# Recurrence of a hybrid decoder step: two squares written with their heads exchanged, summed on the other two 64x64 tiles

## What is computed

```python
kk = k * k_k.astype(f32).reshape(H, N)
kk = kk / jnp.maximum(jnp.sqrt(jnp.sum(kk * kk, axis=-1, keepdims=True)), 1e-12)
...
o, S = _wkv7_scan(S0.astype(f32), r, decay, k, v, kk, a)
mean = jnp.mean(o, axis=-1, keepdims=True)
var = jnp.mean(jnp.square(o - mean), axis=-1, keepdims=True)
o = ((o - mean) * lax.rsqrt(var + LNX_EPS) * lnx_g + lnx_b)
o = o + jnp.sum(r * k * r_k.astype(f32), axis=-1, keepdims=True) * v
```

## Time and profile before

| | us |
|---|---|
| median of 3 runs | 1933.91 |
| lowest and highest of the 3 | 1926.66 and 1935.87 |
| the profiled execution, its own time | 1932.09 |
| its span from the first to the last instruction | 1930.1 |
| busy: PE, PEld, DVE, ACT, POOL | 1802.9, 1538.8, 1049.6, 798.0, 249.6 |
| mean granted clock of TensorE, share of full speed | 0.985 |
| first and last sum over `sq` | 498.9 and 758.9 |
| start of the first `csq`, and of the last | 555.4 and 814.7 |
| `sq`: 16 instructions of ACT, median each | 0.552 |
| `csq`: 16 instructions of ACT, median each | 0.462 |
| one 64x64 weight load, median | 0.135 |
| from one `ss` to the next: a steady slot (643.53 to 659.88) | 16.35 |
| the same for the one long slot among them (607.63 to 627.19) | 19.56 |

### The profile page before, as it was taken

How to read it: one execution, slowest core, us unless ns; L and a number is a source line. 1 busy time by engine, 2 the same in 40 slices (tenths; PEclk the granted TensorE clock), 3 DMA queues, 4 the chain that set the end, 5 groups by cost and what they waited for, 6 DMA issues and landing times.

```text
span 1930.1 us, 43901 instructions
## 1 busy us (share of the span) xinstructions
PE 1802.9 (93%) x18432; PEld 1538.8 (80%) x18432; DVE 1049.6 (54%) x1718; ACT 798.0 (41%) x1459; POOL 249.6 (13%) x315
## 2 busy tenths in 40 slices
PE   7999999999999999999998998999999998778797
PEld 6988999999888888799986776777776776334697
DVE  6744464453588999444445533443463445676334
ACT  4234233233466767333333323233343444555233
POOL 0300000000245555232000000000000001010032
PEclk9999999999999999999999999999999999998899
DMA  8534554555355553243889999999999999999541
GB/s 295 185 142 156 179 180 155 170 179 165 92 137 139 142 137 97 92 141 143 340 292 417 420 419 409 414 426 425 426 426 417 414 425 380 418 393 364 211 146 71
DMA packets 154200, 510.45 MB, mean 264 GB/s; under 512 B 60097, under 2 KB 81986, under 8 KB 108738
## 3 DMA queue, kind: packets, MB, share of 16 engines
q1 hardware_dynamic: 153442, 503.66, 68.8%
q10 hardware_dynamic: 576, 4.19, 0.6%
HBM read 472.86 MB, written 32.32 MB: 262 GB/s over the span
## 4 chain that ended last, share of the span: by engine, by line
PE 31%; DMA 19%; DVE 3%; ACT 2%; issue 2%; SPq 1%; DVEq 0%; ACTq 0%
DMA at_vraw<-in_cache_v 19%; PE psP L2648 8%; PE psP L2650 7%; PE psP L2649 7%; PE at_psO L2702 5%; PE at_psS L2681 3%; SPq L2061 1%; PE psP L2747 0%; DVE wlo L2410 0%; SPq L2101 0%; PE at_psT L2693 0%; DVE at_w L2498 0%; ACT at_p_w L2368 0%; DVE at_p_rc L2593 0%; ACT at_p_w L2366 0%
## 5 line engine op out<-in xcount | busy, mean ns | idle before, releaser
L2648 PE MATMUL psP<-xhi,whi 128*128 128x320 f32 x1488 | 475.3, 319 | 2.9 <-DVE xlo L2535 1.9
L2650 PE MATMUL psP<-xhi,wlo 128*128 128x320 f32 x1488 | 460.7, 310 | 0.0
L2649 PE MATMUL psP<-xlo,whi 128*128 128x320 f32 x1488 | 460.5, 309 | 0.0
L2648 PEld LDWEIGHTS psP<-xhi,whi 128*128 128x128 f32 x1488 | 280.2, 188 | 64.9 <-issue 63.4
L2410 DVE TENSOR_TENSOR wlo<-wraw,whi 128x2048 fp32r<-128x2048 f32 x92 | 212.9, 2314 | 207.7 <-ACT whi L2236 207.5
L2236 ACT ACTIVATE whi<-wraw 128x2048 fp32r<-128x2048 f32 x92 | 176.0, 1913 | 276.7 <-PE psP L2650 275.5
L2649 PEld LDWEIGHTS psP<-xlo,whi 128*128 128x128 f32 x1488 | 280.5, 189 | 0.1
L2650 PEld LDWEIGHTS psP<-xhi,wlo 128*128 128x128 f32 x1488 | 280.3, 188 | 0.0
L139 PE MATMUL psP<-xhi,whi 128*128 128x320 f32 x704 | 218.1, 310 | 2.7 <-DVE wlo L174 2.3
L140 PE MATMUL psP<-xlo,whi 128*128 128x320 f32 x704 | 217.6, 309 | 0.0
L141 PE MATMUL psP<-xhi,wlo 128*128 128x320 f32 x704 | 217.5, 309 | 0.0
(11 more groups left out here) (382 smaller groups left out, 3075.5 us busy)
## 6 DMA issues: line engine op xcount, KB each, us to landing
wraw<-in_weights SPq DMA_DIRECT2D x156, 1024.0 KB, 5.9
at_kraw<-in_cache_k SPq DMA_DIRECT2D x96, 1024.0 KB, 11.1
at_vraw<-in_cache_v SPq DMA_DIRECT2D x94, 1024.0 KB, 10.9
at_kraw<-in_cache_k SPq DMA_DIRECT2D x64, 512.0 KB, 9.8
at_vraw<-in_cache_v SPq DMA_DIRECT2D x62, 512.0 KB, 10.7
rw_s0t<-in_s0T SPq DMA_DIRECT2D x16, 256.0 KB, 3.7
o_wkv_s<-rw_SN SPq DMA_DIRECT2D x16, 256.0 KB, 3.1
wraw<-in_weights ACTq DMA_DIRECT2D x4, 1024.0 KB, 6.5
```

What stands on the lines that cost most here:

```text
L2648: pe.matmul(out, wh, c_.xhi[:, kc, :], start=(kc == 0), stop=False)
L2649: pe.matmul(out, wh, c_.xlo[:, kc, :], start=False, stop=False)
L2650: last = pe.matmul(out, wl, c_.xhi[:, kc, :], start=False, stop=(kc == NM - 1))
```

## The change

The squares are written into the other half of the partitions: what comes from partitions 0 to 63 is written to 64 to 127, and the other way round. [...] The sum then runs with `exchanged=True`: the matmul that reads partitions 0 to 63 (where head 1's squares now lie) writes PSUM partitions 64 to 127, and the other one 0 to 63, so the sums come out where they did before. `bon` and `mean` keep their tiles. `halves` moves from the PE block to the function. `ORDER` is not changed.

```diff
+        halves = [slice(64 * h, 64 * h + 64) for h in range(2)]
...
                     elif name == "sq":
                         loaded(act, "k", t)
-                        F.a.done(act.activation(sq[:], ins["k"][:], ACT.Square, scale=scalar("k_k", t)), name)
+                        for here, there in (halves, halves[::-1]):
+                            squared = act.activation(sq[there], ins["k"][here], ACT.Square, scale=scalar("k_k", t)[here])
+                        F.a.done(squared, name)
...
                     elif name == "csq":
                         R.v.wait(act, "cen", t)
-                        R.a.done(act.activation(csq, cen, ACT.Square), name)
+                        for here, there in (halves, halves[::-1]):
+                            squared = act.activation(csq[there], cen[here], ACT.Square)
+                        R.a.done(squared, name)
...
-            def over_channels(out, mat, x):
-
-                for r in halves:
-                    last = pe.matmul(out[r], mat[r, r], x[r], start=True, stop=True)
+            def over_channels(out, mat, x, exchanged=False):
+
+                for r, to in zip(halves, halves[::-1] if exchanged else halves):
+                    last = pe.matmul(out[to], mat[r, r], x[r], start=True, stop=True)
                 return last
...
-                        F.t.done(over_channels(psF[:, 0:TOK], blk, sq[:]), name)
+                        F.t.done(over_channels(psF[:, 0:TOK], blk, sq[:], exchanged=True), name)
...
-                        R.t.done(over_channels(psR[:, banks_r.of(name), 0:TOK], blkm, csq), name)
+                        R.t.done(over_channels(psR[:, banks_r.of(name), 0:TOK], blkm, csq, exchanged=True), name)
```

More of the change, by code:

```diff
@@ L1563, in _ @@
             pe.wait_ge(masks, c_.n_masks)
-            halves = [slice(64 * h, 64 * h + 64) for h in range(2)]
             def free_p(name, t):
```

## The result

| | before | after |
|---|---|---|
| median of 20 runs each | 1933.51 us | 1940.42 us |
| lowest to highest | 1926.66 to 1944.68 | 1934.39 to 1944.18 |
| ratio to before, 95% interval | | 1.0027, 1.0014 to 1.0040 |
| the profiled execution, own time; span | 1932.09; 1930.1 | 1942.74; 1940.9 |
| `ss` to `ss` in an undisturbed slot | 16.35 | 16.76 |

A forecast was written before the change was run, and what follows sets the result against it. PE is fullest, but waits for ACT and DVE set the pace: +0.1 us over 12 steady tiles and +0.36 in the last make +0.5, so 1932.1 becomes 1932.6, median 1934.4; range 1927 to 1941.

The forecast's parts named there:

- Bound: Steady slot of 16.3 us: PE fullest at 16.10, DVE 15.31, ACT 11.51; the next awaited step decides a pass's worth.
- the freed time is worth little: PE's 0.26 us freed per sum would be spent waiting, after `var` for `U4` and `D2t`, after `ss` for DVE.
- the one ahead of `E`: After `ss`, PE's freed 0.26 us was to become a wait ahead of `Y`, `U2` and `E`.
- the 0.04 named: At `S2`, 0.51 after `E`: a 0.04 us wait for DVE's copy of `SA2` would vanish, won per tile.
- Overlap on PE: At both sums: next matmul starts 0.28 us after the sum starts, not 0.54; 0.26 won on PE per sum.
- Rivals 2 and 3: 2: next matmul stays 0.54 behind sums, 1935.0 or 1938.6, chance 0.12; 3: array drains around exchanged sums, 1942.1 to 1945.3, chance 0.08.
- Rival 1: PE's 0.26 us freed at each of two sums in 13 tiles is won in full: 1927.5 us, chance 0.14.
- rival 4: Stalls move: one gap like the 1.86 us at 614.39 more or less, giving 1931 or 1938 us; chance 0.06.
- The second instruction on ACT: Each square becomes two full-time instructions, neighbours overlapping by 0.10: `csq` costs 0.36 us more, `sq` 0.45; `var` starts 0.06 later.
- The term of +0.01 a tile: Steady tile of the recurrence: +0.05 us at `SA1` less 0.04 at `S2`; 12 tiles make +0.1.
- `sq` off the path: On ACT, the 0.45 us more for `sq` goes into a 1.74 us gap behind `kk0`: cost 0.
- the prediction's last sign: Slots from `ss` to `ss` above 16.6 us would mean ACT's row carries more than seen, `sq` first of all.

## Why the prediction was right or wrong

- **Bound, and "the freed time is worth little": right.** With whole squares the sums gain 0.10 us a slot. New waits stand ahead of `var`, `SA4` and `Y`, as said; the one ahead of `E` does not, as `SA2` (663.51) and `E` (663.63) follow `Y` without a gap. `ss` gains the 0.04 named, but by luck: the premise that `SA2` comes early before `E` fell with that wait, `E` to `S2` is 0.52 against 0.51, and DVE's stretch from `SA1` to `Yt`, of which the prediction said that nothing in it gets shorter, is what got 0.03 to 0.04 shorter.
- **Overlap on PE: right in kind, too small.** The forecast had 0.28 from `var` to the next matmul; it is 0.02. "PE starts in order, so the next one can't start before the second pass" was wrong: the diagonal's matmuls run between the two passes of the sum. It changed nothing, as the time goes into waits. Rivals 2 and 3 (no overlap, a drain) fell with it. Rival 1 (the freed passes are worth their time) fell with the slot of 16.25; it needed 15.9. Of rival 4 one part occurred in the profiled execution, the other way: the long slot was 1.8 us shorter, which is no part of the 0.41 a slot.
- **The second instruction on ACT: mis-sized, and this is the loss.** The step read "Neighbours overlap by 0.10 ... `csq` 0.46 - 0.10 = 0.36 more". It measured 0.62 more to the end of `csq`, and 0.54 more to the start of `U4` where 0.15 was forecast: overlap is gone at three boundaries. Two of them lie in `csq` and make 0.26; the slack before `D2` covered 0.21 as forecast, which leaves 0.41 there; the third, between `D2` and `A12`, adds 0.13. `var` waits 0.30 in place of 0.06; `SA1` is 0.44 late, counted from `Q4`, in place of 0.05. The term of +0.01 a tile is +0.41, and 12 to 13 tiles make 5 us of it. The rows on `sq` showed the overlap between two whole instructions; I took it for a property of the engine.
- **`sq` off the path: right.** It costs more than said: `kk0` starts 1.16 after `sq` in place of 0.45, so 0.70 a tile, and 0.83 with the overlap lost in front of `sq`; all of it in front of a gap of 1.7.
- **Numbers.** 1940.4 lies inside 1927 to 1941, near its end, and within 0.5%, the case given most. But the forecast of 1934.4 with 2 us around it, given 0.60, did not come about, and none of the rivals named ACT's lost overlap. That the time is inside the range is luck: the upper end was set by rivals 2 and 4 and part of 3, none of which made the loss. What did come about is the prediction's last sign: "slots above 16.6 would mean that ACT's row carries more than I saw" - of `csq`, not of `sq`.

## What to carry to other kernels

Time freed on the fullest engine is worth only what the next awaited result allows; in a loop where three engines interlock, follow the two or three awaited steps and their slack before pricing anything. When one instruction becomes two, price the boundaries too: write down for each neighbour whether it still overlaps. And before a step is moved to where its engine has room, look at the transfers that hang on it.

## What was not expected of the hardware

- ACT: neighbours overlap by 0.09 to 0.12 us; an instruction that moves the start partition of its reads or writes from 0 to 64 or back starts 0.01 to 0.03 after its predecessor's end. The Trainium skill, page "ScalarE: Activation LUTs", section "What ACT_TABLE_LOAD costs", has back-to-back instructions overlap by about 93 ns. The trace agrees (0.10) where the start partition stays, and disagrees where it moves. The length does not go by the partitions: `csq` of 64 partitions 0.468, of 128 partitions 0.462.
- PE: two 64x64 tiles that share rows, and two that share columns, work at the same time: four records of `U1`, 0.02 after `var` began, between its passes. The start order is not the program's: the first pass of `ss` (660.84) comes before six records of `D4t` (660.88), which stand ahead of it. The Trainium skill, page "TensorE: Matmul & The Clock Gate", section "The mechanism", has matmuls start strictly in program order, and weight loads pass a running matmul only in other rows. Here both are otherwise: the order of `ss` and `D4t` just named, and the loads of `S1`, which begin at 643.81 in the rows that `ss` still occupies. The Trainium skill, page "TensorEngine Tiling (Array Packing)", section "Key Properties", has independent tiles and no drain on a change of tile. These rows bear it out, as the passes of `D4t` and `S1` stay 0.06 apart while `ss` starts among them.
